# A first stage in written order, a weight ring of 17 slots and later output weights for layer 0, in an eight-core decoder trunk

## The reference

```python
h = rmsnorm(x, pre_g)
u, v, z_a, p, z_b, xc, bg, cg, z_c = split(h @ w_in)      # 6400 columns
vn = rmsnorm(v, v_g)                                      # an output of the sample rows
a_out = u * (masked w_s @ vn + b_s)                       # A: 6 heads, chunks of 128 rows
b_out = ((window mean of p) - p) @ w_pg * pool_scale      # B: 4 groups
c_out = bg * conv3(cg * xc)                               # C: 6 heads
mix = concat(a_out * silu(z_a), b_out * silu(z_b), c_out * silu(z_c))
x = x + rmsnorm(mix @ w_out, post_g)
```

## Time and profile before

| | |
|---|---|
| median of 3 runs | 2041.59 us (2038.41 to 2043.72) |
| the profiled execution, its own time | 2042.29 us |
| its span, from the first to the last instruction, core 7, the slowest | 2041.2 us |
| spans of the 8 cores | 2033.0 to 2041.2 us |
| PE busy on core 7 | 2003.8 us, 98% of the span |
| DVE, ACT, POOL busy | 1170.5, 629.5, 522.4 us |
| share of the chain that ended last | PE 93%, DMA 2%, DVE 2%, issue 2% |

### The profile page before, as it was taken

One profiled execution on the slowest core, in us unless ns is written; L12 is line 12 of the kernel. 1 busy time (PEld: TensorE's weight loads), 2 busy tenths in 40 slices (PEclk: granted clock), 3 DMA queues, 4 the chain that ended last, 5 costly groups with the idle time before them and its releaser, 6 DMA issues.

```text
span 2041.2 us, 38277 instructions; the slowest of 8 cores (2033.0 to 2041.2 us)
## 1 busy us (share of the span) xinstructions
PE 2003.8 (98%) x12288; PEld 1186.2 (58%) x12288; DVE 1170.5 (57%) x1937; ACT 629.5 (31%) x1560; POOL 522.4 (26%) x1032
## 2 busy tenths in 40 slices
PE   6999999999999999999999999999999999999997
PEld 3655565566566466557656546656755655664673
DVE  3754665576565475466575546547657544653763
ACT  3332333323323232232332332323333222232231
POOL 3521421231331131132142123113214212211310
PEclk8999999999999999999999999999999999999999
DMA  9998697788797876859879868686988985758862
GB/s 205 195 191 158 164 211 115 167 150 157 184 182 126 171 162 94 118 147 198 132 198 167 130 167 155 94 158 125 196 166 171 154 123 158 114 82 149 143 114 75
DMA packets 200498, 309.61 MB, mean 152 GB/s; under 512 B 84848, under 2 KB 90096, under 8 KB 198768
## 3 DMA queue, kind: packets, MB, share of 16 engines
q0 software_dynamic: 90912, 174.66, 55.9%
q1 hardware_dynamic: 109104, 131.46, 23.7%
q10 hardware_dynamic: 288, 1.05, 0.2%
HBM read 409.48 MB, written 55.99 MB: 228 GB/s over the span
## 4 chain that ended last, share of the span: by engine, by line
PE 93%; DMA 2%; DVE 2%; issue 2%; ACT 0%; POOL 0%; DVEq 0%; ACTq 0%; POOLq 0%
PE ps L566 61%; PE ps L676 23%; PE ps L536 7%; DMA sb_ring<-w_in 2%; PE ps L763 1%; PE ps L654 1%; DVE sb_pw L386 1%; DMA sb_cstb<-cstb 1%; DVE sb_mix L390 0%; ACT sb_scr L382 0%; DVE sb_scr L390 0%; POOL sb_stats L401 0%; DVE sb_hin L390 0%; DVE sb_xs L386 0%; PE ps L518 0%
## 5 line engine op out<-in xcount | busy, mean ns | idle before, releaser
L566 PE MATMUL ps<-sb_hT,sb_ring 128*128 128x384 bf16 (+1 forms) x8448 | 1329.0, 318 | 9.0 <-DMA sb_ring<-w_in 4.7
L566 PEld LDWEIGHTS ps<-sb_hT,sb_ring 128*128 128x128 bf16 x8448 | 824.7, 98 | 475.8 <-issue 17.9
L382 ACT ACTIVATE sb_scr<-ps 128x384 f32<-128x384 f32 (+3 forms) x664 | 371.1, 563 | 1077.2 <-PE ps L566 508.4
L347 POOL DMA_DIRECT2D sb_ring<-w_in x552 | 296.0, 542 | 919.0 <-PE ps L566 746.8
L676 PE MATMUL ps<-sb_wout,sb_mix 128*128 128x512 bf16 x2176 | 471.6, 379 | 0.0
L676 PEld LDWEIGHTS ps<-sb_wout,sb_mix 128*128 128x128 bf16 x2176 | 212.9, 98 | 255.4
L390 DVE SCALAR_TENSOR_TENSOR sb_scr<-sb_pw,sb_convw,sb_scr 128x384 f32<-128x384 f32 (+1 forms) x336 | 182.1, 542 | 145.3 <-ACT sb_ccarry L382 109.0
L386 DVE TENSOR_TENSOR sb_scr<-ps,sb_scr 128x384 f32<-128x384 f32 (+1 forms) x288 | 151.8, 530 | 131.7 <-PE ps L763 94.9
L399 POOL TENSOR_SCALAR sb_stats<-sb_stats 128x1 f32<-128x1 f32 x204 | 59.0, 289 | 560.0 <-ACT sb_scr L382 555.4
L390 DVE SCALAR_TENSOR_TENSOR sb_hout<-sb_xs,sb_stats,sb_pre_bc 128x1024 bf16<-128x1024 f32 x62 | 79.6, 1284 | 177.7 <-POOL sb_stats L401 177.7
L536 PE MATMUL ps<-sb_ring,sb_hT 128*128 128x512 bf16 (+1 forms) x1088 | 178.8, 326 | 0.0
(11 more groups left out here) (48 smaller groups left out, 501.0 us busy)
## 6 DMA issues: line engine op xcount, KB each, us to landing
sb_ring<-w_in POOLq DMA_DIRECT2D x528, 256.0 KB, 8.5
xd<-sb_xs SPq DMA_DIRECT2D x51, 512.0 KB, 3.5
sb_xs<-xd SPq DMA_DIRECT2D x51, 512.0 KB, 8.6
sb_wout<-w_out POOLq DMA_DIRECT2D x64, 256.0 KB, 12.7
sb_xs<-x_p SPq DMA_DIRECT2D x31, 512.0 KB, 12.0
hd<-sb_hout SPq DMA_DIRECT2D x62, 256.0 KB, 3.9
sb_ring<-w_in POOLq DMA_DIRECT2D x12, 1024.0 KB, 8.4
y_p<-sb_xs SPq DMA_DIRECT2D x16, 512.0 KB, 3.5
```

Of the source, the lines that this page charges most:

```text
L347: emit(POOL, lambda g: g.dma_start(out=flat, in_=src), writes=a.res, dsem=ds, extra=[prev_tok] if prev_tok else [])
L382: return emit(ACT, lambda a: a.activation(out=out, in_=in_, func=func, scale=scale, **kw), reads=reads, writes=writes)
L566: ins = pe.matmul(bank(b, N), lhsT=wa.ap[:, k, :], rhs=hT[:, k, j0 * 128:j0 * 128 + N], start=(k == 0), stop=(k == 7))
```

## The change

Five edits stand together. The first pass is written out job by job: all rows go through SP, with the norm's weights second; every square on ACT stands earlier against the p jobs; 8, 5 and 4 matmuls on zeros follow the first three transposes; and POOL issues p0 when row tile 2 has landed, p1 after tile 3, p2 and p3 after tile 4, the rest behind the norm of tile 4. The ring has 17 slots, whose room comes from `hin`, which now lies in the upper part of `mix`. The sample tile's normed v is written to bf16 straight from PSUM, and a second time to f32 for the output. In the first pass alone the output weights wait: none after the v jobs and the first two heads of A, one after each of the other four heads, three after each of the C heads 0 to 3.

```diff
-NSLOT = 14
+NSLOT = 17
-        hin = sb("hin", [128, NHI, D], BF16)
+        hin = mix[:, 12:16, :].rearrange("p k t -> p (k t)").rearrange("p (s d) -> p s d", s=NHI)
...
+            dve_stt(vn[:, j, :], vps, rs, vg_bc[:], ALU.mult, ALU.mult,
+                    reads=[bank_res[b], bank_res[b + 1], R_stat[si], R["vg_bc"]], writes=[R_vn[j]])
+            if is_s:
                 dve_stt(stg, vps, rs, vg_bc[:], ALU.mult, ALU.mult,
                         reads=[bank_res[b], bank_res[b + 1], R_stat[si], R["vg_bc"]], writes=R_sv)
                 emit(SP, lambda q: q.dma_start(out=vs_o[l], in_=stg), reads=R_sv, dsem=d_vs)
-                dve_copy(vn[:, j, :], stg, reads=R_sv, writes=[R_vn[j]])
...
-                load_pre(0, ACT)
-                sl = [load_x(0, 0), load_x(0, 1)]
-                sl += [load_x(0, 2, ACT), load_x(0, 3)]
+                sl = [load_x(0, 0)]
+                load_pre(0)
+                sl += [load_x(0, 1), load_x(0, 2), load_x(0, 3)]
...
                 warm_up()
+                nr(0)
+                nr(1)
                 sl.append(load_x(0, 4))
+                tj(0, 8)
                 after_x(2)
                 ring_try_alloc()
+                nr(2)
+                sl.append(load_x(0, 5))
+                tj(1, 5)
+                after_x(3)
                 ring_try_alloc()
+                nr(3)
+                tj(2, 4)
                 setup_loads()
                 load_vg(0)
+                pj(0, 0)
+                after_x(4)
+                ring_try_alloc()
+                ring_try_alloc()
+                nr(4)
+                pj(1, 0)
+                tj(3, 0)
+                pump()
+                nr(5)
+                pj(2, 0)
+                tj(4, 0)
+                pj(3, 0)
+                tj(5, 0)
...
-                if wo:
+                if wo and pi > 0:
                     wout_piece(l, wo.pop(0))
...
-                if wo:
+                if wo and (pi > 0 or h >= 2):
                     wout_piece(l, wo.pop(0))
...
-                if wo:
-                    wout_piece(l, wo.pop(0))
+                for _ in range(3 if pi == 0 else 1):
+                    if wo:
+                        wout_piece(l, wo.pop(0))
```

More of the change, by code:

```diff
@@ L430, in warm_up, with fill_pe @@
             emit(DVE, lambda v_: v_.memset(mix[:, 0, 0:512], 0.0), writes=R_mix[0])
+            fill_pe(24)
+        def fill_pe(k):
             def fill(pe):
-                for _ in range(24):
+                for _ in range(k):
                     ins = pe.matmul(bank(7), lhsT=mix[:, 0, 0:128], rhs=mix[:, 0, 0:512], start=True, stop=True)
@@ L553, in v_job @@
                 emit(SP, lambda q: q.dma_start(out=vs_o[l], in_=stg), reads=R_sv, dsem=d_vs)
-                dve_copy(vn[:, j, :], stg, reads=R_sv, writes=[R_vn[j]])
-            else:
-                dve_stt(vn[:, j, :], vps, rs, vg_bc[:], ALU.mult, ALU.mult,
-                        reads=[bank_res[b], bank_res[b + 1], R_stat[si], R["vg_bc"]], writes=[R_vn[j]])
         def in_job(b, wa, sts_i):
@@ L876, in run_pass @@
             if pi == 0:
-                load_pre(0, ACT)
-                sl = [load_x(0, 0), load_x(0, 1)]
-                sl += [load_x(0, 2, ACT), load_x(0, 3)]
+                sl = [load_x(0, 0)]
+                load_pre(0)
+                sl += [load_x(0, 1), load_x(0, 2), load_x(0, 3)]
                 def after_x(k):
-                    POOL.h.wait_ge(d_xs[k].sem, 16)
-                    POOL.waited[id(d_xs[k].sem)] = 16
-                warm_up()
-                after_x(0)
-                ring_try_alloc()
@@ L887, in run_pass, with nr, tj @@
[L887 to L890, removed]
+                    n = 16 * (1 + k // NX)
+                    POOL.h.wait_ge(d_xs[k % NX].sem, n)
+                    POOL.waited[id(d_xs[k % NX].sem)] = n
+                def nr(k):
+                    norm_rows(sl[k], hin[:, k % NHI, :], R_hin[k % NHI])
+                def tj(k, n):
+                    t_job(k, k % NHI)
+                    if n:
+                        fill_pe(n)
@@ L891, in run_pass, with pj @@
+                def pj(gi, si_):
+                    p_job(g, l, gi, si_)
+                warm_up()
+                nr(0)
+                nr(1)
                 sl.append(load_x(0, 4))
-                t_job(0, 0)
+                tj(0, 8)
                 after_x(2)
                 ring_try_alloc()
+                nr(2)
+                sl.append(load_x(0, 5))
+                tj(1, 5)
+                after_x(3)
                 ring_try_alloc()
-                norm_rows(sl[2], hin[:, 2, :], R_hin[2])
@@ L911, in run_pass @@
-                pool_phase(g, l, [(gi, si_) for si_ in range(2) for gi in range(4)], hook)
+                pj(0, 0)
[11 more added lines that the diff above has]
+                tj(5, 0)
+                for gi in range(4):
+                    pj(gi, 1)
+                    release(wsched[(g, l)][("p", gi)])
+                    pool_vec(g, l, gi)
+                    later_pop(2 if gi else 0)
```

## The result

The change makes the kernel slower. Over 19 runs each its median is 2077.44 us against 2042.84, and the ratio is 1.0122 (95% interval 1.0084 to 1.016). Runs in which a whole die was slowed, to a mean clock as low as 0.81, as happens to the kernel before as well, are left out here and in all that follows. The other 15 runs stand on two levels: six from 2050.55 to 2053.15 us, and nine from 2075.51 to 2078.96. In a run of the upper level one pair of cores of a die (2 and 3, or 4 and 5; in one run both pairs) spans 2071 to 2078 us at a mean granted clock of 0.98, and the other cores stand where they stand in the lower level. So two losses are to be explained: some 9 us in every run, and 26 more in most of them. The profiled execution is one of the lower level: its own time 2053.15, span 2052.1 on core 3, the slowest (cores 2036.7 to 2052.1).

A forecast was written before the change was run, and what follows sets the result against it. The DMA engines, full for nearly the whole first pass, were taken as the bound. Out stage +9.6, clock +2.6 and sample's v 0 gave +12.2 us on 2041.2; forecast 2054 us, range 2041 to 2063.

The forecast's parts named there:

- the clock's price: Out stage: after PE's idle the clock drops as after the earlier C wait, costing 2.6 us (0 to 4).
- the sum: Whole span: 9.6 + 2.6 + 0 = +12.2 us on 2041.2, so 2053.4.
- out stage starts later: Out stage of the first pass: starts at 185.1 us (175.1 + 2 + 8), 9.6 later than before.
- The four more pieces ahead of the last output piece: POOL's queue: 58 slots instead of 54 land first, four pieces at 1.58 us, 6.3 us; last landing at 175.1.
- Nothing is taken from the queue: POOL's weight queue: the deferred output pieces are only moved behind other weights, so its backlog does not shrink.
- The order of issue: POOL's queue: its DMAs land in the order in which they were issued.
- The queue's later start and the transposed loads: Weight queue: first weights issued some 4 us later, +2 (-3 to +4); next group's transposed loads hold it, +8 (0 to 13).
- The first stage: Start of the first pass: v jobs begin at 38 us (31 to 44) instead of 44.4.
- The rival that the change does not do what it says at the start: First stage: tile 5 held, v jobs at 44 as before, PE arrives at 168 not 162, time hardly moves; no chance given.
- The ring at nothing: Later passes: a deeper ring has no weight wait to remove, costed at nothing; its harm, v0's place, counted elsewhere.
- The sample's v at 0: Heads of A in three layers: first wait gains at most 0.67 us each, can lose 0.45; taken as 0 (-2 to +1.4).
- PE's idle at the out stage: Before the first out job: PE arrives at 161.8 us and idles over 15 us for an output piece.

The follow-up runs named there:

- e4: The change, but no weight piece of the next pass is fetched until all 16 output pieces are issued; 2041.0 us, ratio 1.0000 to the kernel before.
- e2: The kernel before with only the later output weights of layer 0 (14 slots, old first stage); 2048.1 and 2048.0 us, ratio 1.0034.
- m1: The kernel before with the later output weights and the ring of 17 slots (old first stage, old sample's v); 2046.9 us, ratio 1.0043.
- g3: The kernel before with the ring of 17 slots and e4's order of output and next-pass weights; 2037.2 us, ratio 0.9984.
- k1: e4 with the old sample's v, p0 to p3, v0, v1 issued behind row tiles 0 to 3, `w_pg` and SP's later loads behind v1; 2045.7 us, ratio 1.0004.
- g2: The kernel before with the ring of 17 slots alone, its room taken from `mix`; 2044.9 us, ratio 1.0018.
- e3: The change with 32 matmuls of unused result on PE ahead of the first out job; 2047.8 and 2048.0 us, ratio 1.0032.
- g1: The change as it is, run again; its profile caught a run of the upper level, 2080.98 us.
- h2: g3 with PE waiting, ahead of the out stage, for the next group's first transposed load; 2059.4 us, ratio 1.0073.

## Why the prediction was wrong

It said slower, and 2054 us; the kernel is slower, and the median is 2077.44, outside the range of 2041 to 2063.

**The step that failed is the clock's price.** "I add the clock's price after the earlier wait, 2.6 us (0 to 4)" was sized on one wait of 4.7 us in the C stage, and with that row it is right for the lower level: 44.07 - 41.60 = 2.5 us. In 13 of 34 runs, and in 9 of the 15 counted in the first set, some 26 us more were lost: in the run that was traced, 161 us at a clock of 0.81 behind the same restart, about 30 us. The range had no case for it, and what brings it stays open. The lower level, 2050.6 to 2053.2, lies 1 to 3 us under the sum.

**That the sum of the lower level came so near was luck: its terms were not right.** From core 7 before to core 3 after the span grew by 10.9 us, against 12.2 predicted:

| term | predicted | measured |
|---|---|---|
| out stage starts later | +9.6 | +3.4 (178.91 against 175.49) |
| clock behind the wait | +2.6 | +2.5 |
| sample's v and what follows to the last out stage | 0 | +5.0 (1828.2 - 1820.7 - 2.5) |

The +3.4 sets one core against another. Core 7's wait for C was the longest before (4.7 us, against 0.5 to 2.9 on the others); on core 3 itself the out stage starts 8.2 us later (170.75 before).

- The four more pieces ahead of the last output piece: predicted landing 175.1 us, measured 178.7 on core 3 (the out stages of the eight cores start at 170.3 to 178.9). e4 bears out the count. "Nothing is taken from the queue" does not hold with 14 slots, as e2 shows; in the change the larger ring makes it true (3.11 MB from 60 to 80 us on core 3). The order of issue held: in the kernel before, the change, e2 and m1 each of a core's 552 ring DMAs landed behind the one issued before it. The Trainium skill, "DMA: Bandwidth & Descriptors", Two DMAs through the same engine are not ordered, says that nothing orders DMAs across the engines; no ring DMA of these runs showed it.
- The queue's later start and the transposed loads: predicted +2 and +8, measured together +3.6 on core 3, which landed last. Behind a full weight queue it is the transposed loads that wait, 22 us each, with 13.7% of the engines to the weights' 91.9%. The Trainium skill, "Advanced Engine Details and Errata", X-Bar Transpose (TRN2), by which transposing DMAs are no slower than others, was nearer to this case than the earlier trace rows, though by another way than its rate.
- The first stage: predicted v jobs at 38 us, measured 45.6 on core 3. The rival that the change does not do what it says at the start came true. It cost nothing at the end, as that rival has it, since PE waits at the out stage anyway. Where PE does not, it shows: e4's out stages start at 168.7 to 172.1 us, those of g3, with the old start, at 166.1 to 168.8. k1 shows that the written order can give 35 to 40 us for the v jobs, and that on most cores the pass's bytes then take it back.
- The ring at nothing: wrong in its parts, since g2 lost 3 us. It took away the C wait by itself and brought the waits for `w_pg` and for the last piece; only the last was counted. That it also keeps the queue full when output pieces are deferred (m1 against e2) was not counted either.
- The sample's v at 0: the first wait fell as said, and the cost behind it was +1.1 us on core 7 (1821.8 from out stage to out stage, against 1820.7) and 5.0 on core 3, which had the wait for the f32 store's buffers that no term held; not all of the 5.0 is shown to be the edit's.
- PE's idle at the out stage: predicted over 15 us, measured 2.7 to 9.6, because PE arrived at 168 to 173 in place of 161.8 and the piece earlier.

## What to carry to other kernels

Where the DMA engines are full for a whole stage, a piece moved back makes another one late. Count the pieces ahead of the last one that a stage needs, and hold back what the next stage wants until it is issued: that alone was worth 10 us here, and with the old start it beat the kernel before. Look, too, at what a deferred load leaves behind: in e2 the queue ran empty where the load had stood. A wait that PE meets before a dense stage can cost more than its length (2.5 us more behind 8.4 here), and a few useless matmuls in its place can be the cheaper choice (3 us in e3).

## What the runs showed of the hardware

- A third level of TensorE's granted clock, 0.81, on one pair of cores for 161 us, beginning some 5 us behind the return to the full clock (one traced run, g1).
- The price of an idle in the clock behind it did not grow with its length: 2.5 us behind 8.4 on core 3 of the change, 1.4 behind 22.0 on core 0 of h2, and none behind 2.7 and 3.4 on cores 6 and 7 of the change (41.60 us each).
- SP stays in the issue of transposed loads while the DMA engines are full: 44.8 us for six of them on core 6 of k1, with every later DMA of its queue behind them.
